# Latents first, context second at five norm boundaries of a two-block diffusion trunk on one NeuronCore

## The reference

```python
def rmsnorm(x, w):
    x32 = x.astype(jnp.float32)
    r = lax.rsqrt(jnp.mean(x32 * x32, axis=-1, keepdims=True) + EPS)
    return (x32 * r).astype(x.dtype) * w
def modulate(h, shift, scale):
    return h * (1 + scale) + shift
def swiglu(h, w_i, w_o):
    g, u = jnp.split(h @ w_i, 2, axis=-1)
    return (jax.nn.silu(g) * u) @ w_o
...
    xl = xl + 0.5 * g1l * swiglu(modulate(rmsnorm(xl, norm_w[0]), sh1l, sc1l), w_ffn1_in, w_ffn1_out)
    xc = xc + 0.5 * g1c * swiglu(modulate(rmsnorm(xc, norm_w[0]), sh1c, sc1c), w_ffn1_in, w_ffn1_out)
    hl = modulate(rmsnorm(xl, norm_w[1]), sh2l, sc2l)
    hc = modulate(rmsnorm(xc, norm_w[1]), sh2c, sc2c)
```

## Time and profile before

| | |
|---|---|
| median of 3 runs | 4289.51 us (4289.47 to 4299.35) |
| the profiled execution | 4287.59 us |
| its span, first to last instruction | 4285.8 us |
| mean granted clock of PE | 0.993 |
| PE busy | 4187.1 us, 98% of the span |
| PE weight loads | 3729.0 us, 87% |
| DVE busy | 3071.4 us, 72% |
| ACT busy | 1793.0 us, 42% |
| POOL busy | 1331.9 us, 31% |

### The profile page before, as it was taken

The page is one execution under the profiler, slowest core; times in us unless marked ns, Lnnn a source line. Parts: engine busy times, 40 slices in busy tenths (PEclk is TensorE's granted clock), DMA queues, the critical chain, the costliest instruction groups (busy, mean ns, idle before and its releaser), DMA issues.

```text
span 4285.8 us, 61414 instructions
## 1 busy us (share of the span) xinstructions
PE 4187.1 (98%) x24279; PEld 3729.0 (87%) x24279; DVE 3071.4 (72%) x4936; ACT 1793.0 (42%) x2976; POOL 1331.9 (31%) x699
## 2 busy tenths in 40 slices
PE   7999999999999999999999999999999999999999
PEld 5888778888888799867999999999999799998887
DVE  5775558877887686465599798788887675554776
ACT  3233352233233544263234786333334645444444
POOL 0000200000000100000378666777772058444443
PEclk9999999999999999999999999999999999999999
DMA  7543215544555364212477899999994166678884
GB/s 276 221 165 146 84 43 203 223 179 191 220 194 203 109 253 184 79 40 77 142 243 250 301 342 343 367 359 353 358 352 166 60 199 220 226 245 285 288 287 168
DMA packets 287199, 926.35 MB, mean 216 GB/s; under 512 B 19648, under 2 KB 171328, under 8 KB 212800
## 3 DMA queue, kind: packets, MB, share of 16 engines
q1 hardware_dynamic: 250048, 788.18, 51.8%
q0 software_dynamic: 36864, 134.23, 8.7%
HBM read 837.40 MB, written 84.93 MB: 215 GB/s over the span
## 4 chain that ended last, share of the span: by engine, by line
PE 86%; DVE 5%; DMA 4%; ACT 2%; POOL 1%; issue 1%; SPq 0%; ACTq 0%; POOLq 0%; DVEq 0%
PE bank L1132 25%; PE bank L1133 24%; PE bank L1134 24%; PE bank L1570 3%; DMA gates<-work 1%; PE bank L1325 1%; PE bank L1127 1%; PE bank L1122 1%; PE bank L1118 1%; PE bank L1337 1%; POOL weight_ring_low L2906 1%; PE bank L1362 1%; DVE work L2635 1%; DVE weight_ring_low L2246 1%; DMA work<-in_up_rows,work 1%
## 5 line engine op out<-in xcount | busy, mean ns | idle before, releaser
L2906 POOL TENSOR_TENSOR weight_ring_low<-weight_ring,up_high 128x1024 fp32r<-128x1024 f32 x233 | 586.4, 2521 | 1069.7 <-ACT up_high L1994 1067.6
L1134 PE MATMUL bank<-peer_h_high,weight_ring_low 128*128 128x256 f32 (+2 forms) x2240 | 698.3, 312 | 0.0
L1132 PE MATMUL bank<-peer_h_high,up_high 128*128 128x384 f32 (+1 forms) x2048 | 643.4, 314 | 14.3 <-POOL weight_ring_low L2906 7.4
L1133 PE MATMUL bank<-h_low,up_high 128*128 128x384 f32 (+1 forms) x2048 | 633.8, 309 | 0.0
L2081 ACT ACTIVATE down_high<-weight_ring 128x1024 fp32r<-128x1024 f32 x256 | 257.1, 1052 | 523.5 <-PE bank L1134 518.0
L1134 PE MATMUL bank<-h_high,weight_ring_low 128*128 128x512 f32 (+1 forms) x1280 | 463.9, 362 | 0.0
L1132 PE MATMUL bank<-h_high,in_high 128*128 128x512 f32 (+1 forms) x1216 | 441.1, 363 | 0.3
L1133 PE MATMUL bank<-h_low,in_high 128*128 128x512 f32 (+1 forms) x1216 | 440.8, 362 | 0.0
L2870 POOL TENSOR_SCALAR h<-work,params 128x256 f32<-128x256 f32 x12 | 11.8, 997 | 1376.7 <-PE bank L1477 874.6
L2662 DVE TENSOR_TENSOR weight_ring_low<-weight_ring,down_high 128x1024 fp32r<-128x1024 f32 x128 | 314.8, 2459 | 160.8 <-ACT down_high L2081 160.8
L1134 PEld LDWEIGHTS bank<-peer_h_high,weight_ring_low 128*128 128x128 f32 x2240 | 426.4, 190 | 3.7
(11 more groups left out here) (417 smaller groups left out, 10074.5 us busy)
## 6 DMA issues: line engine op xcount, KB each, us to landing
weight_ring<-in_up SPq DMA_DIRECT2D x128, 1024.0 KB, 6.0
weight_ring<-in_down SPq DMA_DIRECT2D x128, 1024.0 KB, 5.6
weight_ring<-in_mod_w SPq DMA_DIRECT2D x112, 1024.0 KB, 4.8
weight_ring<-in_ffn_in SPq DMA_DIRECT2D x88, 1024.0 KB, 6.9
weight_ring<-in_ffn_out SPq DMA_DIRECT2D x64, 704.0 KB, 5.7
gates<-work SPq DMA_DIRECT2D x40, 1024.0 KB
gelu<-work SPq DMA_DIRECT2D x64, 384.0 KB
work<-gates SPq DMA_DIRECT2D x32, 768.0 KB, 12.8
```

The costliest lines, as they stand in the source:

```text
L1132: mm(dst, w_high, a_high, start=first, stop=False)
L1133: mm(dst, w_high, a_low, start=False, stop=False)
L1134: return mm(dst, w_low, a_high, start=False, stop=last)
L2906: G.tensor_tensor(ring_low[:, slot, w], ring[:, slot, w], up_high[:, n % 3, :].bitcast(F32), ALU.subtract)\
```

## The change

For the stages where 512 tokens follow a joined product ("half"), the last panel is made in two halves of 256 columns, the latents' in its own bank and the context's in bank 5 (halved_panel). Between them stand the column sums of the total so far, and among the terms of the context half the sums of the latents' last square and the spreading of the latents' scales. ACT and DVE normalise the latents in that time (halved_norm, halved_end), into places of their own; first_products becomes halved_products, which makes the latents' columns of the four blocks in three passes (high, low, low weights) and then the context's. The fillers of these boundaries are gone. DVE takes the low parts of weight units 0 and 1 after the latents' low parts and ahead of all scaled context chunks. The high parts of units 0 and 1 get places of their own (first_unit).

```diff
+        first_units = dict(
+            ffn_ffn=((FC + 12) * T, 0), ffn_mix=(0, 18 * T), mix_ffn=(shared_at, shared_at + UNIT), even_peer=(shared_at, shared_at + UNIT))
...
+            def halved_products(name, s, blocks):
...
+                for kc in range(KC):
+                    pe.wait_ge(half_rounded, m0 + kc + 1)
+                    for bank, k, j0, cols in blocks:
+                        mm(ps[bank][:, LAT], unit_block(k, j0 + kc), high[:, kc, LAT], start=kc == 0, stop=False)
+                    if kc == 3:
+                        pe.wait_ge(squares_ready, at[norm]["square"] + KC)
+                        column_sums(ns, norm, (2, 3), False, True).then_inc(summed, 1)
+                for kc in range(KC):
+                    pe.wait_ge(half_split, m0 + kc + 1)
+                    for bank, k, j0, cols in blocks:
+                        mm(ps[bank][:, LAT], unit_block(k, j0 + kc), h_low[:, kc, LAT], start=False, stop=False)
+                    if kc == 1:
+                        pe.wait_ge(inverse_ready, at[norm]["norm"] + 1)
+                        spread_scales(ns["late_scale"], (2, 3)).then_inc(panel_done, 1)
+                low_block = lambda k, j: ring_low[:, weight_unit(name, s, k) % SLOTS, w(j)]
+                for bank, k, j0, cols in blocks:
+                    pe.wait_ge(in_split, r0 + k + 1)
+                    for kc in range(KC):
+                        i = mm(ps[bank][:, LAT], low_block(k, j0 + kc), high[:, kc, LAT], start=False, stop=kc == KC - 1)
+                    if cols == TL:
+                        i.then_inc(panel_done, 1)
+                blocks = [b for b in blocks if b[3] == T]
...
+            def halved_panel(before, early_bank, terms, part, first_half=None):
+
+
+                norm, ns = before
+                last = len(terms) - 1
+                for n, term in enumerate(terms):
+                    o = split_product(ps[early_bank][:, LAT], *part(term, LAT), n == 0, n == last)
+                o.then_inc(half_done, 1)
+                pe.wait_ge(squares_added, at[norm]["joined"] + KC - 2)
+                column_sums(ns, norm, range(4), True, False).then_inc(summed, 1)
+                for n, term in enumerate(terms):
+                    o = split_product(ps[ns["late_bank"]][:, CTX], *part(term, CTX), n == 0, n == last)
+                    if n == first_half:
+                        o.then_inc(out_half, 1)
+                    if n == (len(terms) + 3) // 4:
+                        pe.wait_ge(half_squared, ns["half"] + 1)
+                        column_sums(ns, norm, (0, 1), False, True).then_inc(half_summed, 1)
+                    if n == len(terms) // 2:
+                        pe.wait_ge(half_inverted, ns["half"] + 1)
+                        spread_scales(ns["scale_bank"], (0, 1)).then_inc(half_spread, 1)
+                o.then_inc(panel_done, 1)
...
+            def halved_norm(name, s):
...
+                act.wait_ge(half_added, n + 1)
+                act.wait_ge(summed, at[name]["summed"] + 1)
+                total, kc = squares_of(name, s, KC - 1), s["order"][KC - 1]
+                A(total[:, LAT], x[:, kc, LAT], ACT.Square).then_inc(half_squared, 1)
+                round_unit(*s["next"], 0)
+                act.wait_ge(half_summed, n + 1)
+                root(slice(0, 2), half_rooted)
+                for kc in range(KC):
+                    act.wait_ge(half_scaled, n * KC + kc + 1)
+                    normalise(half_h[:, kc, :], high[:, kc, LAT], kc, 0, half_normed, half_rounded, n * KC + kc + 1)
+                    if kc == 3:
+                        act.wait_ge(x_added, at[name]["added"])
+                        A(total[:, CTX], x[:, s["order"][KC - 1], CTX], ACT.Square).then_inc(squares_ready, 1)
+                    if kc == 5:
+                        act.wait_ge(summed, at[name]["summed"] + 2)
+                        root(slice(2, 4), root_ready)
+                for kc in range(KC):
+                    act.wait_ge(scaled_ready, at[name]["scaled"] + kc + 1)
+                    normalise(h[:, kc, CTX], high[:, kc, CTX], kc, 1, normed, h_rounded, at[name]["normed"] + kc + 1)
+                round_unit(*s["next"], 2)
...
+            def halved_norm(name, s):
...
+                for kc in range(5):
+                    half_low(kc)
+                dve.wait_ge(root_ready, at[name]["root"] + 1)
+                V.reciprocal(norm_scale[:, 2:4], square_sum[:, 2:4]).then_inc(inverse_ready, 1)
+                for kc in range(5, KC):
+                    half_low(kc)
+                split_unit(*s["next"], 0)
+                split_unit(*s["next"], 1)
+                dve.wait_ge(panel_done, plan.panel0[name] + 1)
+                for kc in range(KC):
+                    V.tensor_tensor(h[:, kc, CTX], x[:, kc, CTX], ps[s["late_scale"]][:, CTX], ALU.mult).then_inc(scaled_ready, 1)
+                    if kc >= 3:
+                        low(kc - 3)
...
```

139 lines of the change are left out of this document (131 added, 8 removed).

## The result

| | before | the change |
|---|---|---|
| median | 4293.68 us (4284.57 to 4301.73, 10 runs) | 4307.58 us (4299.78 to 4317.37, 10 runs) |
| ratio, 95% interval | | 1.0034 (1.0023 to 1.0045) |
| the profiled execution | 4287.59 us | 4305.55 us |
| its span | 4285.8 us | 4303.7 us |
| mean granted clock of PE | 0.993 | 0.991 |

What follows compares the result with a forecast made beforehand. TensorE, with matmuls in flight for 98% of the span, was taken as the bound. From 4287.6 us, waits of 30.0 against 21.2 won add 8.8 and clock falls 4.2, giving 4300.6 us, range 4292 to 4311.

Steps and rivals of the forecast that it cites:

- pauses of the last FFN panel: Boundaries 1, 3 and 4: PE waits 1.2, 6.3 and 5.2 us for DVE's last join of squares.
- other waits: PE's waits for ACT's pace, the spread at mixers and boundary 4's end, 17.3 us of the 30.0 in all.
- Won minus added: All five boundaries: 44.2 us taken away, less 9.0 for splits and 14.0 for sums and spreads, wins 21.2 without waits.
- (a) The join: Column sums after the latents' half wait for DVE's last join of squares: 1.2, 0, 6.3, 5.2, 0 us at boundaries 1-5.
- (b) ACT's pace: Scaled chunks each 0.95 us make PE wait 1.6 us per FFN panel, 4.1 per mixer's, plus 0.75 at the mixer's spread.
- (c) Boundary 4's end: Boundary 4: context pass at ACT's pace costs 1.1 us, the third weight unit's late rounding and low part 1.85.
- (d) The clock: Granted clock falls behind the pauses of boundaries 3 and 4, priced 2.1 us each, 4.2 for two.
- The lengths forecast: Before the clock: boundary 1 about 0.6 us shorter, 2 and 5 about 0.8 longer, 3 some 4.5 and 4 some 3 longer.
- No wait at the join: Rival: DVE comes to the join sooner, so 11.5 us of waits and 4.2 of clock go: 4284.9 us; chance 0.09.
- The clock falls at all five: Rival: clock falls at all five boundaries or longer; three more falls give 4306.9 us, longer ones up to 4311; chance 0.17.

Runs made afterwards that it cites:

- The kernel with both causes away: The change with PE awaiting the last weight unit's second half only where used, and six instead of seven modulation units beside FFN out-panels: ratio 0.9989.
- the interleaving: PE's latents' high and low passes interleaved, low three chunks behind, on the kernel with both causes away plus earlier ACT weight roundings: 4279.92 us, ratio 0.9966.
- the last version: The interleaved kernel with unit 1's low part taken behind three scaled context chunks at boundary 4 alone: one of three versions of 4279 to 4284 us.
- the run with the late wait: The change, but PE waits for the FFN's last weight unit's second-half low part only ahead of the terms using it: 4312.75 us, ratio 1.0039.
- the early rounding: The kernel with both causes away, with ACT rounding unit 0 earlier at mixers and the third unit between latents' and context's chunks: 4287.09 us, ratio 0.9987.
- the kernel with six units alone: The change with six instead of seven modulation units beside the FFN's out-panels and nothing else: ratio 1.0035 (1.002 to 1.0051).
- the run with fillers: The change with six filler matmuls between PE's waits for the two halves of the FFN's last weight unit: 4302.33 us, ratio 1.0026.

## Why the prediction was right, and where not

The forecast was 4300.6 us within 4292 to 4311, that is 1.0030 of its base; the ratio is 1.0034 (1.0023 to 1.0045), clear of no change, and just over the prediction's bound of 0.3% with an interval that lies on both sides of it. The prediction gave 0.46 to slower by more than the bound and 0.47 to less, so it had not decided between the two. By the boundary lengths its total was 8.8 + 4.2 = 13.0 us and 14.2 were measured, but part of that agreement is luck, since its terms were off by more, in both directions:

```
term (us)                                forecast   measured
won if PE never waited                      -21.2      -19.9
pauses of the last FFN panel                 12.7       12.6
other waits                                  17.3       14.7
clock                                         4.2        6.8
sum                                          13.0       14.2
```

Step by step:

- **Won minus added (21.2 us).** About 1.3 too high. The kernel with both causes away lies 5.2 us under before. The waits left in it are 0.94 at each of boundaries 1 and 3 (the interleaving's gain); 3.6 at boundary 4 (40.51 down to 37.37 in the last version, which still has 0.48 ahead of the next product, 1363.32 to 1363.92); and at each mixer 0.64 for the spread and 4.0 for the pace (0.78 ahead of the first group, from 613.30 to 614.20 above less the spacing of 0.12; 1.80 that the interleaving gave; and three chunks at 0.94 - 0.48 that it left). They add up to 14.7, so without waits 19.9 us would be won. What the sum lacked is the step from the context half to the first product, 0.76 - 0.12 = 0.64 us at each of boundaries 1, 3 and 4, where the trace puts its idle time down to issue: 1.9 in all. At the mixers the trace puts that gap down to ACT. That is 0.6 more than the difference, so the rest of the sum was off by that much the other way, and no run says in which term.
- **(a) The join.** The mechanism and the sizes were right for a kernel that this one is not: 1.00, 6.13, 5.04 us in the run with the late wait. In the change itself the waits are 0, 2.61 and 0.2.
- **The missed step.** "I take the start of the last panel as 0", and "PE makes the latents' half in 66 x 0.12 = 7.9 us": I let the halved panel start as the old one did. It waits for the low parts of both halves of the last weight unit ahead of its first term. ACT rounds the second half only when PE is done with panel 6, and DVE takes its low part behind that. That is 3.28 us at each of three boundaries, 9.8 in all. It took the place of most of the 12.7 us forecast for the join, since it pushes PE back while DVE goes on. These waits together came to 9.8 + 2.8 = 12.6 us: the number was right by luck and its mechanism half wrong. At boundary 1 they were 3.3 us against the 1.2 forecast, at 3 5.9 against 6.3, and at 4 3.5 against 5.2. The wait stands in the code ahead of the call of halved_panel; I read the function and not its caller.
- **(b) ACT's pace.** 0.94 us per chunk, as said. At FFN boundaries 0.94 was lost instead of 1.6 (measured at 1 and 3; at 4 the same is assumed), at mixers 4.0 + 0.64 instead of 4.1 + 0.75. The mixers lost 0.42 each, forecast 0.8.
- **(c) Boundary 4's end.** The third unit cost 1.95 us (from the end of the first products at 1389.57 to 1391.52; 1.85 forecast), of which the early rounding gave back 1.47. If the latents' pace costs 0.94 at this boundary as at 1 and 3, the context's pace cost 3.14 - 1.47 - 0.94 = 0.73 (1.1 forecast); the two were not measured apart, the last order change gave their 1.67 together.
- **(d) The clock.** It fell at three boundaries instead of two, at 1 because of the missed pause. With the kernel without pauses as the base, the falls cost 49.36 - 43.15 - 3.28 = 2.93 us at boundary 1, 51.03 - 43.15 - 3.28 - 2.61 = 1.99 at 3, and 45.84 - 40.51 - 3.27 - 0.2 = 1.86 at 4. The price of 2.1 each was near; the count was wrong, 6.8 us instead of 4.2.
- **The lengths forecast.** Boundary 1 was to be 0.6 us shorter and was 4.1 longer; the run with the late wait has it 0.7 shorter. Boundary 3, 5.8 longer (4.5 and 2.1 for the clock forecast), boundary 4, 3.5 (3 and 2.1).
- **The rivals.** "No wait at the join" would have been 4284.9 us. With six units and the late wait the ratio is 0.9989 of before, 4.7 us under it, against the 2.7 below the profiled execution's time that was forecast for it. "The clock falls at all five" was wrong at 2 and 5: PE at ACT's pace, with four matmuls and 0.20 us shown idle in each 0.94 us, kept 1.00.

## What to carry to other kernels

When a product is cut into halves, every wait that stood between its terms must be placed again: one that was hidden behind the first terms is exposed if it moves to the front. Two waits on one engine that stand one behind the other can hide each other; removing either showed little here (0.4 and 3.7 us in sum) and both together the whole (19.4 us), so a term that "gives nothing" is to be tried again with the next one removed. And where a whole kernel's scatter is as large as the effect, lengths between two fixed points of the trace, with the stretches between them as a check, show to tenths of a microsecond what the medians leave open. A fall of the clock between the two points goes into the length, and the next section shows that the same pause does not always bring it.

## What the runs showed of the hardware

- The same pause doesn't always bring the clock down. Behind the pause of 3.28 us at boundary 3 the change had 1.00 (window 976 to 980 above), and the kernel with six units alone 0.51 at the same place:

```profile
976.00:978.00 2.00, 2.00 (x12) 2.00 (x11) 0.06 (x1) 0.00 (x0) 0.00 (x0) 0.51 0.98 414
```

  Its cost varied too: 2.93 and 2.71 us at boundary 1, 1.72 at 3, 1.86 and 1.48 at 4. The Trainium skill (TensorE: Matmul & The Clock Gate, Part 1: The HAM clock gate) says that the activity watch runs freely and doesn't start with the kernel's own work; by that rule a pause costs more or less by where it falls, and these rows agree with it, though they don't show it by themselves.
- At the boundaries, the shortest idle stretch that was followed by a fall was the wait of 1.58 us in the run with fillers, at boundary 4. At the end of boundary 4 of the change, PE idle for 1.80 us, no fall was seen, nor at the 0.48 to 1.00 us elsewhere. Between boundaries 1 and 2 all fourteen kernels have the same pause of 1.79 us (586.22 in the change, 581.10 before); a fall follows it in seven of them and not in the other seven, these two among them. In the five of the seven that also have the fall behind the pause of 1.75 us some 16 us earlier, as the kernel before has it, this stretch takes 181.5 to 181.9 us instead of 180.2.
- The clock also falls with no idle time at all. In the kernel before, and at the same place in all fourteen, PE makes 64 matmuls of one column in a row, and the clock falls in the middle of them:

```profile
1692.12:1695.72 3.60, 3.60 (x33) 3.60 (x33) 3.10 (x6) 3.44 (x7) 0.00 (x0) 1.00 0.51 214
1695.72:1702.67 6.95, 6.95 (x34) 6.86 (x33) 0.00 (x0) 0.00 (x0) 0.00 (x0) 0.50 0.00 0
```

  So PE shown as busy is no proof that the clock stays up. The groups of 8 and 4 such matmuls at the boundaries were followed by no fall where no pause stood with them.
- Twelve filler matmuls with nothing to compute saved 2.76 us at boundary 1, without the panel starting any sooner.
- A first matmul behind column sums or a spread comes 0.20 us ahead of its follower instead of 0.12. Five groups a boundary (0.82 for the eight sums and 0.36 each for the other four, plus 0.08 each) make 2.7 us, against the 2.8 that the prediction had from a count of twelve at the old spacing.
